# One plain tile pair instead of two in the first FFN matrix, and the adaLN gate of the FFN summed by ScalarE and an accumulating DMA

## The reference

```
mod = silu(c) @ w_ada + b_ada
sh_m, sc_m, gt_m, sh_f, sc_f, gt_f = split(mod, 6)      # 1024 values each
...
h = rmsnorm(x, norm_pre_ffn) * (1 + sc_f) + sh_f
gate, up = split(h @ w_ffn_in, 2)                       # w_ffn_in 1024 x 5632
y = (silu(gate) * up) @ w_ffn_out                       # w_ffn_out 2816 x 1024
x = x + gt_f * rmsnorm(y, norm_post_ffn)
```

## Time and profile before

| | us |
|---|---|
| median of three runs | 678.06 |
| profiled execution | 679.46 |
| its span | 677.7 |
| PE busy in the span | 664.1 (98%) |
| DVE busy | 592.8 (87%) |
| ACT busy | 378.5 (56%) |
| POOL busy | 159.3 (23%) |

### The profile page before, as it was taken

How to read it: one execution, slowest core, us unless ns; L and a number is a source line. 1 busy time by engine, 2 the same in 40 slices (tenths; PEclk the granted TensorE clock), 3 DMA queues, 4 the chain that set the end, 5 groups by cost and what they waited for, 6 DMA issues and landing times.

```text
span 677.7 us, 12901 instructions
## 1 busy us (share of the span) xinstructions
PE 664.1 (98%) x4580; PEld 557.0 (82%) x4580; DVE 592.8 (87%) x976; ACT 378.5 (56%) x647; POOL 159.3 (23%) x129
## 2 busy tenths in 40 slices
PE   7999999999999998999999999999999999999996
PEld 6566578777786876888878899999999998888885
DVE  4887989898898988989897599999999998999686
ACT  7367664646564443644773355555555657655544
POOL 4000000000000000000004366866766743521100
PEclk9999999999999998999999999999999999999999
DMA  9973222232223357658334245435434437999703
GB/s 280 357 218 97 62 64 63 63 124 62 63 63 97 122 187 260 217 189 288 100 103 146 71 118 149 120 107 151 137 111 123 128 117 141 190 255 293 150 2 124
DMA packets 104350, 96.82 MB, mean 143 GB/s; under 512 B 2975, under 2 KB 87027, under 8 KB 104310
## 3 DMA queue, kind: packets, MB, share of 16 engines
q1 hardware_dynamic: 98870, 85.82, 41.2%
q0 software_dynamic: 5440, 10.49, 9.0%
HBM read 94.20 MB, written 2.10 MB: 142 GB/s over the span
## 4 chain that ended last, share of the span: by engine, by line
PE 62%; DVE 6%; issue 2%; DMA 1%; ACT 1%; DVEq 0%; SPq 0%; ACTq 0%
PE ps L2424 27%; PE ps L2472 16%; PE ps L1894 8%; PE ps L1913 3%; PE ps L1931 3%; PE ps L2238 1%; DMA w_raw<-in_w_in 1%; DVE w_lo L1143 1%; PE ps L2258 1%; DVE act L1558 1%; PE ps L2395 1%; PE ps L2402 1%; PE ps L1952 1%; DVE act L1561 1%; PE ps L2397 1%
## 5 line engine op out<-in xcount | busy, mean ns | idle before, releaser
L1894 PE MATMUL ps<-h_hl,w_hi 128*128 128x512 f32 x544 | 175.2, 403 | 0.0
L1894 PEld LDWEIGHTS ps<-h_hl,w_hi 128*128 128x128 f32 x544 | 98.9, 189 | 26.0 <-issue 6.0
L1894 PE MATMUL ps<-h_hl,w_lo 128*128 128x512 f32 x272 | 106.5, 392 | 0.0
L2424 PE MATMUL ps<-h_hl,w_hi 128*128 128x256 f32 x576 | 104.5, 283 | 0.0
L2472 PE MATMUL ps<-w_hi,ht_hl 128*128 128x512 f32 x312 | 96.2, 389 | 0.0
L2424 PEld LDWEIGHTS ps<-h_hl,w_hi 128*128 128x128 f32 x576 | 90.0, 192 | 0.2
L2424 PE MATMUL ps<-h_hl,w_lo 128*128 128x256 f32 x288 | 81.5, 283 | 0.0
L2424 PE MATMUL ps<-ht_hl,w_hi 128*128 128x256 f32 x432 | 78.6, 283 | 0.0
L2472 PEld LDWEIGHTS ps<-w_hi,ht_hl 128*128 128x128 f32 x312 | 58.6, 188 | 12.1
L2424 PEld LDWEIGHTS ps<-ht_hl,w_hi 128*128 128x128 f32 x432 | 67.4, 192 | 0.0
L1143 DVE TENSOR_TENSOR w_lo<-w_raw,w_hi 128x1024 fp32r<-128x1024 f32 (+1 forms) x50 | 58.4, 1175 | 6.4 <-ACT w_hi L611 5.8
(11 more groups left out here) (336 smaller groups left out, 1353.8 us busy)
## 6 DMA issues: line engine op xcount, KB each, us to landing
w_raw<-in_w_ffn_in SPq DMA_DIRECT2D x44, 512.0 KB, 4.6
w_raw<-in_w_in SPq DMA_DIRECT2D x28, 512.0 KB, 3.9
w_raw<-in_w_ffn_out POOLq DMA_DIRECT2D x14, 512.0 KB, 7.5
act<-in_w_ada SPq DMA_DIRECT2D x12, 512.0 KB, 8.1
adaw<-in_w_ada SPq DMA_DIRECT2D x6, 1024.0 KB, 5.7
act<-in_w_ada SPq DMA_DIRECT2D x6, 1024.0 KB, 5.2
res<-in_x SPq DMA_DIRECT2D x8, 512.0 KB, 5.7
w_raw<-in_w_out SPq DMA_DIRECT2D x8, 512.0 KB, 4.9
```

Of the source, the lines that this page charges most:

```text
L1894: last = mm(ps[bank][0:rows, :], a, b, start=(k == 0 and n == 0), stop=(k == KT - 1 and n == 2))
L2424: last_mm = mm(ps[bank][:, 0:HALF], a, b, start=(start and k == 0 and n == 0), stop=(k == 3 and n == 2), skip_group_check=not start)
```

## The change

`FIRST_PAIR` goes from 2 to 1, so pair 1 is made by the half-size products too, and `feature_group` is called for two groups only (L2402 and on: the loop over u = 0 to 3 goes). The start-up orders of ACT and DVE are written anew for this. The work on the gate moves: ACT copies the column of `silu(c)` and scales `tail_slot` in place (`scale_tail`, behind snapshot p1 of tile (i, 0)); POOL adds it to `sum_gate_ffn` by an accumulating DMA from SBUF to SBUF (`add_tail(i - 1)`, behind the sums of tile (i, 0)), and SP waits for that DMA ahead of the load of block i. The split of the finished gate moves behind pair 9 on ACT and behind tile (10, 0) on DVE.

```diff
-PAIRS, FIRST_PAIR = FT // 2, 2
+PAIRS, FIRST_PAIR = FT // 2, 1
...
+TAILS = 16 * 8
+ADDED_BASE = (TAILS, 0, 0, 0)
...
             def load_tail(i):
-                wait_apart(sum_used, i + (SUMS - 1))
+                if not isinstance(i, int):
+                    wait_apart(added[0], i * 16 - 16)
                 sp.dma_start(tail_slot, w_ada[0][ds(i * P - P, P), 5 * D_MODEL:6 * D_MODEL]).then_inc(sum_loaded[0], 16)
...
             load_tail(1)
-            for v in range(2):
-                for half in range(2):
-                    sp.wait_ge(lo_ok, G_WIN - 3 + 2 * v + half)
-                    load_fin(FIRST_PAIR, v, half)
-            load_tail(2)
             with sp.Fori(FIRST_PAIR + 1, KT + 1) as i:
                 load_win(i)
                 load_tail(i)
...
-            sp.wait_ge(sum_used, SUMS + KT)
+            sp.wait_ge(added[0], TAILS)
             load_fout((1, 0))
...
-            with pool.Fori(FIRST_PAIR + 1, PAIRS) as i:
+            def add_tail(i):
+
+                pool.wait_ge(tail_k, i * 2)
+                pool.sem_inc(pool_waits, 1)
+                pool.dma_start(sum_gate_ffn, tail_slot, accum_op=ALU.add).then_inc(added[0], 16)
+
+            pool.wait_ge(gate_bias, 32)
+            with pool.Fori(FIRST_PAIR + 1, KT + 2) as i:
+                weight_sums(i, 0, False)
+                weight_sums(i, 0, True)
+                add_tail(i - 1)
+                weight_sums(i, 1, False)
+                weight_sums(i, 1, True)
+            for i in range(KT + 2, PAIRS):
                 for v in range(2):
                     weight_sums(i, v, False)
                     weight_sums(i, v, True)
...
+            def scale_tail(i):
+
+                sc.wait_ge(sum_loaded[0], i * 16 + 16 * (SUM_LOADS // 2))
+                sc.activation(silu_k[:, :], silu_pad[:, ds(i * 32 - 32, 1)], ACT.Copy).then_inc(tail_k, 1)
+                sc.wait_ge(tail_k, i * 2 - 1)
+                sc.activation(tail_slot, tail_slot, ACT.Copy, scale=silu_k[:, 0:1]).then_inc(tail_k, 1)
...
                 snap(p1, 0)
+                if tail:
+                    scale_tail(i)
                 next_hi(0)
...
             plain_silu(0, 0)
-            split_hi(0, U_FIN[0] + 1, G_FIN + 1)
-            split_hi(1, U_FIN[1] + 1, G_FIN + 2)
             feature_sum_hi(0)
+            win_hi(FIRST_PAIR, 0, 0)
+            feature_sum_hi(1)
+            win_hi(FIRST_PAIR, 0, 1)
+            feature_sum_hi(2)
+            win_hi(FIRST_PAIR, 0, 2)
             plain_silu(0, 1)
...
             win_hi(FIRST_PAIR, 0, 3)
             feature_sum_hi(3)
-            win_pair(FIRST_PAIR)
+            win_pair(FIRST_PAIR, True)
             with sc.Fori(FIRST_PAIR + 1, KT + 1) as i:
-                win_pair(i)
-            sc.wait_ge(sum_used, SUMS + KT)
-            sc.activation(first_hi[:, :], sum_gate_ffn, ACT.Copy).then_inc(gate_hi_ok, 1)
+                win_pair(i, True)
             for i in range(KT + 1, PAIRS - 1):
                 win_pair(i)
+            sc.wait_ge(added[0], TAILS)
+            sc.activation(first_hi[:, :], sum_gate_ffn, ACT.Copy).then_inc(gate_hi_ok, 1)
...
-            def add_tail(i):
-
-                ve.wait_ge(sum_loaded[0], i * 16 + 16 * (SUM_LOADS // 2))
-                V.tensor_copy(silu_k[:, :], silu_pad[:, ds(i * 32 - 32, 1)]).then_inc(tail_k, 1)
...
             feature_sum(0)
             plain_swiglu(0, 0)
-            split_lo(G_FIN + 4, 0)
-            split_lo(G_FIN + 5, 1)
             feature_sum(1)
+            win_lo(FIRST_PAIR, 0, 0)
             feature_sum(2)
             feature_sum_lo(0)
+            feature_sum_lo(1)
+            win_lo(FIRST_PAIR, 0, 1)
+            feature_sum(3)
+            feature_sum_lo(2)
+            win_lo(FIRST_PAIR, 0, 2)
             plain_swiglu(0, 1)
...
             win_lo(FIRST_PAIR, 0, 3)
             feature_sum_lo(3)
-            win_pair(FIRST_PAIR, add_tail)
-            with ve.Fori(FIRST_PAIR + 1, KT + 1) as i:
-                win_pair(i, add_tail)
-            win_pair(KT + 1, last_lo)
+            win_pair(FIRST_PAIR)
+            with ve.Fori(FIRST_PAIR + 1, PAIRS - 1) as i:
+                win_pair(i)
             win_tile(PAIRS - 1, 0, lambda u: win_lo(PAIRS - 1, 1, u))
+            gate_lo()
             win_tile(PAIRS - 1, 1, fout_lo, True)
...
                     feature_group(G_FIN + u, u, u)
-                for u in range(4):
-                    te.wait_ge(act_ok[u // 2], 1)
-                    feature_group(G_FIN + 4 + u, u, u)
```

More of the change, by code:

```diff
@@ L309, in build @@
         stored = sem("stored")
-        sp_waits, ve_waits, te_waits = sem("sp_waits"), sem("ve_waits"), sem("te_waits")
+        sp_waits, ve_waits, pool_waits = sem("sp_waits"), sem("ve_waits"), sem("pool_waits")
         block = ctx.enter_context(nc.Block())
@@ L573, in weight_sums @@
                 gate_w, up_w = w_raw[2 * v], w_raw[2 * v + 1]
-                if isinstance(i, int) and v == 0:
+                if isinstance(i, int) and i == FIRST_PAIR and v == 0:
                     if not last_two:
@@ L599, in _ @@
                 if n >= 4:
-                    pool.wait_ge(added[n % 4], n // 4 * 16)
+                    pool.wait_ge(added[n % 4], ADDED_BASE[n % 4] + n // 4 * 16)
                 pool.dma_start(by_pair(out_raw[RAW_OF[kind, q]]), fout_block(q, ADD_TO[kind]), accum_op=ALU.add
@@ L1019, in win_hi, with win_tile @@
                 sc.activation(w_hi[u][:, 0:src.shape[1]], src, ACT.Copy).then_inc(hi_ok, 1)
-            def win_tile(i, v, next_hi):
+            def scale_tail(i):
[3 more added lines that the diff above has]
+                sc.activation(tail_slot, tail_slot, ACT.Copy, scale=silu_k[:, 0:1]).then_inc(tail_k, 1)
+            def win_tile(i, v, next_hi, tail=False):
                 bank = 4 - 4 * v
@@ L1050, in win_tile, with win_pair @@
                 next_hi(3)
-            def win_pair(i):
-                win_tile(i, 0, lambda u: win_hi(i, 1, u))
+            def win_pair(i, tail=False):
+                win_tile(i, 0, lambda u: win_hi(i, 1, u), tail)
                 win_tile(i, 1, lambda u: win_hi(i + 1, 0, u))
@@ L1088, in fout_hi @@
                 if use in ADDED_AS:
-                    sc.wait_ge(added[ADDED_AS[use] % 4], ADDED_AS[use] // 4 * 16 + 16)
+                    sc.wait_ge(added[ADDED_AS[use] % 4], ADDED_BASE[ADDED_AS[use] % 4] + ADDED_AS[use] // 4 * 16 + 16)
                 else:
@@ L1235, in add_sum @@
                                            op1=ALU.add).then_inc(sum_used, 1)
-            def add_tail(i):
-                ve.wait_ge(sum_loaded[0], i * 16 + 16 * (SUM_LOADS // 2))
-                V.tensor_copy(silu_k[:, :], silu_pad[:, ds(i * 32 - 32, 1)]).then_inc(tail_k, 1)
-                ve.wait_ge(tail_k, i)
-                ve.wait_ge(sum_used, i + (SUMS - 1))
-                V.scalar_tensor_tensor(out=sum_gate_ffn, in0=tail_slot, scalar=silu_k[:, :], in1=sum_gate_ffn,
-                                       op0=ALU.mult, op1=ALU.add).then_inc(sum_used, 1)
             ve.wait_ge(consts, 1)
@@ L1815, in win_tile, with win_pair, gate_lo @@
                     fout_act_lo(3)
-            def win_pair(i, more):
+            def win_pair(i):
                 win_tile(i, 0, lambda u: win_lo(i, 1, u))
-                more(i)
                 win_tile(i, 1, lambda u: win_lo(i + 1, 0, u))
-            def last_lo(i):
+            def gate_lo():
                 ve.wait_ge(gate_hi_ok, 3)
@@ L1840, in _ @@
             plain_swiglu(0, 0)
-            split_lo(G_FIN + 4, 0)
-            split_lo(G_FIN + 5, 1)
             feature_sum(1)
+            win_lo(FIRST_PAIR, 0, 0)
             feature_sum(2)
             feature_sum_lo(0)
-            plain_swiglu(0, 1)
-            split_lo(G_FIN + 6, 2)
-            split_lo(G_FIN + 7, 3)
-            feature_sum(3)
-            feature_sum_lo(1)
-            feature_sum_lo(2)
-            plain_swiglu(1, 0)
-            win_lo(FIRST_PAIR, 0, 0)
-            ve.wait_ge(gate_bias, 32)
-            add_tail(1)
-            win_lo(FIRST_PAIR, 0, 1)
-            plain_swiglu(1, 1)
-            win_lo(FIRST_PAIR, 0, 2)
+            feature_sum_lo(1)
[3 more added lines that the diff above has]
+            win_lo(FIRST_PAIR, 0, 2)
+            plain_swiglu(0, 1)
             win_lo(FIRST_PAIR, 0, 3)
             feature_sum_lo(3)
-            win_pair(FIRST_PAIR, add_tail)
-            with ve.Fori(FIRST_PAIR + 1, KT + 1) as i:
-                win_pair(i, add_tail)
-            win_pair(KT + 1, last_lo)
+            win_pair(FIRST_PAIR)
+            with ve.Fori(FIRST_PAIR + 1, PAIRS - 1) as i:
+                win_pair(i)
             win_tile(PAIRS - 1, 0, lambda u: win_lo(PAIRS - 1, 1, u))
+            gate_lo()
             win_tile(PAIRS - 1, 1, fout_lo, True)
```

9 lines of the change are left out of this document (removed).

## The result

| | before | after |
|---|---|---|
| median, us | 678.0 (677.91 to 678.65) | 703.25 (702.59 to 703.48) |
| profiled execution / its span | 679.46 / 677.7 | 703.28 / 701.5 |
| mean granted clock of PE | 0.997 | 0.992 |

The change costs 25.25 us: a ratio of 1.0364, with [1.0352, 1.0377] as its 95% interval. The forecast was +17.8 us, with 683 to 711 us as its range. The spans of the two profiled executions differ by 23.8 us, which is what a trace can account for. The profiled execution of before lies 1.5 us above its median, that of after on it.

The account below looks back on a forecast made before the run. PE alone was taken to bound the stretch, without gaps. Matmul saving -1.6, start-up +0.6, pair 2 +5.0 and pairs 3 to 8 +13.8 sum to +17.8 us: 695.9 us from 678.06, range 683 to 711.

Parts of the forecast that it names:

- PE bounds, so each gap is paid in full: From 351.4 to 564 us PE alone bounds without gaps, so any gap the change opens costs its full length.
- The round, its links and where it bites: One `tail_slot` through POOL, DMA, SP, ACT: ends T+28.25, PE wants T+25.92 (T: pair's first matmul); 2.3 us gap, pairs 3 to 8.
- The terms of the round: POOL's sums T+15.4, issue 0.2, accumulation 5.9, SP 0.25, block load 3.7, ACT 2.8 us: T+28.25.
- the quiet row: Profile row of an accumulating DMA from HBM with queues quiet, 512 KB in 6.0 us; the prediction took 5.9.
- Pair 2: DVE behind after the start-up: round ends 393.65, PE wants the snapshot at 388.65; gap 5.0 us, bounds 2 and 8.
- The start-up: Pair 1: ACT's snapshot p1 ready at 365.5, PE wants it at 365.0; gap 0.6 us, bounds 0 and 2.
- The rest just holds: Pair 1 behind its first gap: the remaining needs of PE, to 367.3, 369.0 and 371.0, are just met, without another gap.
- the slow accumulation: Rival: accumulating DMA takes 8 us, as among other transfers; 2.1 us more in each of seven pairs, 710.6 us; chance 0.08.
- What costs nothing: ACT's 1.3 and POOL's 1.2 us a pair fit; first tail load, held weight loads, gate's split and extra transfer cost nothing.
- DVE's relief buys nothing: DVE loses a block's additions, about 2.2 us a pair; no time bought by itself, since PE doesn't wait for DVE.
- the quick accumulation: Rival: accumulating DMA as quick as a plain load, 3.7 us: 680.5 us, chance 0.07; 0.5 us shorter still, 679.4, 0.04.
- The gapless case: Rival: quick accumulation and early POOL sums also in pair 2, so only PE's 1.6 us saving shows: 676.5 us; chance 0.03.

## Why the prediction was right, and where its sizes were off

*PE bounds, so each gap is paid in full*: right. The stage grew by 18.3 (gaps of pairs 2 to 8), 2.6 (start-up), 4.5 (clock) and 0.7 (the steps behind gaps), less 1.6: 24.5 us, and 24.6 were measured. The 23.8 of the spans are these less the 0.7 us by which the part ahead ended sooner.

*The round, its links and where it bites*: right, and shown from both sides. Taken out at POOL's end or at ACT's end, the gaps go; put into the kernel before, they come. PE waits where the sum said, at its third x product in the first tile of each pair, for ACT's snapshot.

*The terms of the round.* The link that was mis-sized most is the accumulation: 5.9 us were taken from the quiet row. It took 6.3 to 7.0 for the gaps of the pairs 3 to 8, with a weight load issued 0.9 us ahead of it; with one issued 2.6 us ahead alone it took 4.6 to 5.5 (6.2 once), and 4.5 with none under way. The prediction counted weight loads as company for the tail load but not for the accumulation. Yet the gaps of these pairs are 2.5 us each, for 2.3 forecast. Pair 3 shows what made up for it. The chain of waits of after:

```profile
403.21 7.03 DMA res<-tail_place
410.49 3.98 DMA tail_place<-in_w_ada
```

Pair 2 began at 384.55 and ran for 24.64 us instead of 20.16, by its gap and the slow matmuls. Had POOL been carried along by all of these 4.5 us, its issue would have stood at T+20.1; it came at T+18.66. POOL was 1.4 us earlier, the accumulation 1.1 and the load 0.3 longer, and the gap was 2.3, to the tenth what was forecast. POOL's issue held it for 0.86 to 0.88 us (1.06 the first time), not 1.2, which changed nothing.

*Pair 2*: forecast 5.0 us, the largest gap by far; measured 3.1. The end of its round was right to 0.2 us (393.44 for 393.65), in part by luck: POOL issued 1.1 us later than forecast (382.08 for 381.0), and the accumulation took 4.9 us for 5.9. The other end was not: PE came to the place at 390.3 and not at 388.65, because it had lost more in the start-up. A gap is a difference of two times, and time that is lost ahead of it is taken out of it.

*The start-up*: forecast 0.6 us, measured 2.6. The gap ahead of p1 was seen (0.82 for 0.6), with its cause. The second one wasn't: 1.11 us ahead of the product y of slot 3, for the last low part of a feature sum. "The rest just holds" said 371.0, and this low part ended at 372.4; DVE's row, beside POOL's sums, has nearly twice the 1.18 us of a low part alone:

```profile
370.09 2.31 DVE L1710 TENSOR_TENSOR h_hl<-act,h_hl 128x1024 fp32r<-128x1024 f32 x1
```

This term is 2.0 us short.

*The clock* isn't in the sum at all. It is the largest error: 4.5 us of slow matmuls, of which some 1.2 may have come back as shorter stops, as the run with the idle matmuls suggests. The rows of before had the clock at 1.00 and no gap, so nothing in them priced a gap of 2 to 3 us beyond its length. The range held it by the slow accumulation's side, for another reason.

*All gaps together*: the pairs 2 to 8 give 18.3 us, forecast 18.8. That is partly luck, as pair 2 was put too large and the others a little too small. The stage's error is 6.8 us, 24.6 for 17.8. Of these, 4.5 (clock), 2.0 (start-up) and 0.7 (the steps behind gaps), less 0.5 (the gaps) give 6.7 of them. By the medians the error is 7.5 us.

*What costs nothing*: right. With the accumulation early, ACT's scaling, POOL's issue and the additional transfer cost no time that the comparison with the kernel without blocks could show (679.64 for both). *DVE's relief buys nothing*: right to about 1 us. The kernel without blocks and the one with the blocks on DVE differ by 0.3 us in the median and 1.3 in the stage.

*The rivals*: the quick accumulation wanted 3.7 us, and no accumulation of any run landed in under 4.5; in the pairs 3 to 8 of this kernel none landed in under 6.3. The gapless case is excluded by the table of waits.

None of the versions is faster than the kernel before. The best of the new ones are 0.2% slower: the 1.6 us of the matmul change are less than what its start-up costs. Whether an order exists that keeps POOL's sums and both low parts in time is open; with the three orders tried, pair 1 had a gap of 2.40 to 2.81 us in its second tile instead of two of about 1 us.

## What to carry to other kernels

When a buffer goes round through several engines in order, add up one whole round, waits in each queue included, and set it against the period of the engine that bounds. Moving the start of the round (POOL issues half a pair sooner) or its end (ACT scales behind the snapshots) gave back over 20 us with the same instructions. A wait for a transfer on an in-order engine belongs behind whatever the bounding engine needs from it next. And price a gap on PE with the clock behind it: the matmuls slowed by it cost here a quarter of the stops' own length (4.5 us for 18.3), with the round alone some 40% (6.0 for 14.4).

## What the runs showed of the hardware

- The granted clock fell to its lower level for some 3 us behind three of seven gaps in the changed kernel: those of 2.97, 2.77 and 2.39 us. It stayed at 1.00 behind one of 2.86 us, and with the round alone it fell behind one of 1.88. So the length of the gap alone doesn't decide, and the runs don't show what does. Small matmuls in the gap kept it at 1.00.
- An accumulating DMA of 512 KB from SBUF to SBUF landed in 4.5 us with no other load under way (the scaling moved behind the snapshots), in 4.6 to 5.5 with a weight load issued 2.6 us earlier (6.2 once), and in 5.9 to 7.1 with a second one issued 0.9 us earlier. Its issue held POOL for 0.86 to 0.89 us, the first time in a kernel for 1.06.
- A POOL instruction of 512 columns took 1.3 us alone, 2.2 in turns with DVE, and 4.48 and 6.22 beside unbroken series of DVE instructions whose inputs were both in SBUF.
